# Values projected beside the tasks of the pair ahead and transposed, queries and keys in turn, FFN's rows behind its residuals

## What is computed

```python
proj = h @ w_in                      # queries, keys and values of all 16 heads, and the forget logits
s = einsum('bqhd,bkhd->bhqk', q, k) / sqrt(64) + F_q - F_k      # F: running sum of log_sigmoid
p = softmax(where(kpos <= qpos, s, NEG))
x = x + g1 * (einsum('bhqk,bkhd->bqhd', p, v) @ w_o)
...
u = h @ w_up                                                     # 1024 -> 5632
gate, val = split(conv_b + sum(conv_w[j] * shifted(u, j) for j in range(3)))
x = x + g2 * ((silu(gate) * val) @ w_down)
```

## Time and profile before

| what | us |
|---|---|
| median of 3 runs | 2390.47 (2387.61 to 2393.91) |
| the profiled execution | 2388.44 |
| its span, first to last instruction | 2386.6 |
| PE busy in it | 2293.8 (96%) |
| DVE, ACT, POOL busy | 1541.0, 1146.3, 1209.4 |

### The profile page before, as it was taken

How to read it: one execution, slowest core, us unless ns; L and a number is a source line. 1 busy time by engine, 2 the same in 40 slices (tenths; PEclk the granted TensorE clock), 3 DMA queues, 4 the chain that set the end, 5 groups by cost and what they waited for, 6 DMA issues and landing times.

```text
span 2386.6 us, 30699 instructions
## 1 busy us (share of the span) xinstructions
PE 2293.8 (96%) x10986; PEld 1909.2 (80%) x10986; DVE 1541.0 (65%) x2536; ACT 1146.3 (48%) x1993; POOL 1209.4 (51%) x1641
## 2 busy tenths in 40 slices
PE   5999999998998999999999999989999999999998
PEld 4778788787877888888888878987778888888886
DVE  6565756658789677777776577882775555555556
ACT  5365664746255333333333496771553333333333
POOL 1501312133557666667666562214376666666663
PEclk9999999999999999999999999989999999999999
DMA  6211211114621333344332323233111111111112
GB/s 264 63 49 36 69 38 50 45 45 176 222 96 58 111 124 124 124 128 124 121 123 93 106 71 78 54 109 130 36 45 53 54 53 53 54 53 54 54 54 80
DMA packets 69082, 207.20 MB, mean 87 GB/s; under 512 B 7729, under 2 KB 8369, under 8 KB 68802
## 3 DMA queue, kind: packets, MB, share of 16 engines
q1 hardware_dynamic: 35248, 121.13, 15.7%
q10 hardware_dynamic: 33682, 84.11, 11.0%
HBM read 186.92 MB, written 16.32 MB: 85 GB/s over the span
## 4 chain that ended last, share of the span: by engine, by line
PE 80%; DVE 12%; ACT 4%; issue 2%; DMA 1%; SPq 0%; ACTq 0%; DVEq 0%
PE bank L1063 50%; PE bank L753 18%; PE bank L892 1%; PE bank L918 1%; PE bank L953 1%; PE bank L928 1%; PE bank L1280 1%; PE bank L955 1%; PE bank L954 1%; PE bank L1220 1%; DVE ada_raw L1974 1%; DMA ada_raw<-in_ada_t 1%; ACT H L1405 1%; DVE bank L2064 1%; DVE PL L2090 1%
## 5 line engine op out<-in xcount | busy, mean ns | idle before, releaser
L1063 PE MATMUL bank<-H,w_spl 128*128 128x512 f32 x3552 | 824.2, 390 | 8.2 <-DVE X L2285 6.5
L1063 PEld LDWEIGHTS bank<-H,w_spl 128*128 128x128 f32 x3552 | 667.6, 188 | 151.8 <-DVE X L2285 9.3
L651 POOL TENSOR_TENSOR w_spl<-w_raw,w_spl 128x256 fp32r<-128x256 f32 x688 | 551.3, 829 | 408.1 <-ACT w_spl L1647 406.7
L1063 PE MATMUL bank<-TB,w_spl 128*128 128x512 f32 x2112 | 493.6, 390 | 1.6 <-DVE TB L2245 1.6
L753 PE MATMUL bank<-H,w_spl 128*128 128x512 f32 x1920 | 481.3, 397 | 5.2 <-DVE H L2424 2.5
L1063 PEld LDWEIGHTS bank<-TB,w_spl 128*128 128x128 f32 x2112 | 396.1, 188 | 85.8 <-issue 3.4
L753 PEld LDWEIGHTS bank<-H,w_spl 128*128 128x128 f32 x1920 | 354.7, 190 | 76.2 <-DVE H L2424 2.9
L1647 ACT ACTIVATE w_spl<-w_raw 128x512 fp32r<-128x512 f32 x328 | 196.4, 624 | 348.0 <-PE bank L1063 291.8
L590 POOL TENSOR_TENSOR pace<-one_s 128x1 f32<-128x1 f32 x49 | 13.7, 280 | 578.9 <-PE bank L918 352.4
L2276 DVE TENSOR_TENSOR bank<-bank,sU 128x512 f32<-128x512 f32 x80 | 55.9, 699 | 280.7 <-PE bank L1063 280.7
L2285 DVE SCALAR_TENSOR_TENSOR X<-bank,mods,X 128x1024 f32<-128x1024 f32 x160 | 204.7, 1279 | 34.6 <-PE bank L1063 33.9
(11 more groups left out here) (203 smaller groups left out, 3367.7 us busy)
## 6 DMA issues: line engine op xcount, KB each, us to landing
w_raw<-in_w_stream SPq DMA_DIRECT2D x184, 512.0 KB, 3.7
ada_raw_f<-in_ada_t ACTq DMA_DIRECT2D x136, 256.0 KB, 2.9
ada_raw<-in_ada_t SPq DMA_DIRECT2D x8, 1024.0 KB, 18.8
negF<-scratch_f ACTq DMA_DIRECT2D x16, 512.0 KB, 3.8
ada_raw_o<-in_ada_t ACTq DMA_DIRECT2D x4, 2048.0 KB, 8.1
ada_raw_o<-in_ada_t ACTq DMA_DIRECT2D x4, 1536.0 KB, 8.0
Hf<-scratch_o ACTq DMA_DIRECT2D x9, 512.0 KB, 4.5
X<-in_x_t SPq DMA_DIRECT2D x4, 1024.0 KB, 11.7
```

Source lines behind the costliest of these rows:

```text
L651: last = pool.tensor_tensor(block_at(layer, b, 1, q, q + 256), src[:, q:q + 256], block_at(layer, b, 0, q, q + 256).bitcast(F32), ALU.subt ...
L1063: last = pe.matmul(dst, block_at(layer, b, x, k * P, k * P + P), mov(y), start=(start and x + y == 0), stop=(stop and x == 1), skip_group_ ...
```

## The change

**Values.** They are projected for each pair from the third on, with the weights as the stationary operand: `v_step(r, i)` is half of a product of 128 value columns by 256 rows of the sequence, 12 matmuls of 256 columns, and stands in task 14 + i of the pair before (i from 0 to 7). The result is transposed: ACT copies a quarter of 256 rows out of PSUM (`copy_vt`, a task behind), PE transposes it in two (`turn_v`, two tasks behind), and ACT and DVE split it (`v_high`, `v_low`, three tasks behind). The weight tiles are laid out for it, one more stationary tile per pair in place of two moving ones per group. Nothing stands between groups any more.

**Queries and keys.** From the third pair on the halves come in turn: queries and keys of the first half of the sequence, then of the second. A table `FILL` is the same for every pair but the first. All heads have their maxima beside the tasks of the head before (`MAX_T`).

**Heads' outputs.** They may come into H when the last values are projected, not the last keys; `HEADS_SPLITS` and `OUT_A_BESIDE` start later.

**ConvFFN.** In pair 2 the four rows of factors go behind the gating and the third residual, the first residual stands right behind the first taps; in pair 3 the first row goes behind a sum. ACT's two loads for it stand at the end of pair 2.

In the diff comments and empty lines are left out.

```diff
-MAX_V = [0, 0, 0, 3, 3, 3, 3, 0]
-MAX_K = (1, 4, 7)
-MAX_T = [[2, 1, 1, 1, 1, 1, 1, 2, 2, 0, 0, 0], [0, 0, 2, 1, 2, 1, 2, 1, 2, 1, 0, 0]]
-MAX_T.append(MAX_T[0])
-V_EARLY = 3
-V_TASK = 4 * NT - V_EARLY
+MAX_T = [[2, 1, 1, 1, 1, 1, 1, 2, 2, 0, 0, 0], [1, 1, 1, 1, 1, 1, 2, 1, 2, 1, 0, 0]]
+MAX_T += MAX_T
 PREFACE = 16
-FILL_1 = [2] * 16
-FILL_1_FIRST = [2] * 8
-FILL_2 = [0] * (2 * NT) + [1, 1, 1, 1, 1, 2] * 2 + [3, 2, 2, 2] * 2
+FILL = [3, 2, 2, 3, 2, 2, 2, 2, 2, 3, 3, 3, 3]
+FILL_FIRST = [2] * 8
+V_TASK = 14
...
-HEADS_SPLITS = {22: 0, 24: 1, 26: 2, 28: 3, 30: 4, 32: 5, 42: 6}
+HEADS_SPLITS = {26: 0, 27: 1, 29: 2, 31: 3, 33: 4, 35: 5, 42: 6}
...
-OUT_A_BESIDE = {25: (0,), 28: (1,), 31: (2,), 34: (3,), 37: (4,), 40: (5,), 44: (6,)}
+OUT_A_BESIDE = {28: (0,), 30: (1,), 32: (2,), 34: (3,), 37: (4,), 40: (5,), 44: (6,)}
...
-    return (n % 2, n // 2) if n < 4 else (n % 4 // 2, n % 2)
+    return (n % 4 // 2, n % 2) if n // 4 == 1 else (n % 2, n % 4 // 2)
 def qk_pos(n):
     pair = n // 4
-    if pair == 0:
-        return 2 + n % 2
-    return 6 * (pair // 2) + 4 * (pair % 2) + n % 4 // 2
+    return 2 * (pair == 0) + 3 * pair + (pair == 1) + qk_part(n)[0]
 def qk_steps(g, T):
-    if T < 2 * NT:
-        fill, done, first = (FILL_1, 0, 8 * g + 4) if g else (FILL_1_FIRST, PREFACE, 4)
-    elif g < NG - 1:
-        fill, done, first = FILL_2, 0, 8 * g + 8
-    else:
+    r, t = 2 * g + T // (2 * NT) + 1, T % (2 * NT)
+    fill, done = (FILL, 0) if r > 1 else (FILL_FIRST, PREFACE)
+    if 2 * r >= NH or t >= len(fill):
         return []
-    if T >= len(fill):
-        return []
-    a = done + sum(fill[:T])
-    return [(first + i // KT, i % KT) for i in range(a, a + fill[T])]
+    a = done + sum(fill[:t])
+    return [(4 * r + i // KT, i % KT) for i in range(a, a + fill[t])]
+def v_beside(g, T):
+    q, t = divmod(4 * NT * g + T, 2 * NT)
+    return [(q + 1, t - V_TASK)] if 0 <= t - V_TASK < 8 and 1 <= q < NH // 2 - 1 else []
+def v_quarter(g, T):
+    return [(r, i // 2) for r, i in v_beside(g, T) if i % 2]
...
-                            sp.wait_ge(qk_ps, 8 * NG)
+                            sp.wait_ge(v_ps, 8 + 4 * (NH // 2 - 2))
...
-            def v_step(g, tt, between=True):
...
+            def v_step(r, i):
+                qd = i // 2
+                if i == 0:
+                    pe.wait_ge(w_ready, 3 * r + 3)
+                if i in (0, 2):
+                    pe.wait_ge(qk_lo, 2 * (4 * r + 3 + qd))
+                elif i % 2 == 0:
+                    pe.wait_ge(v_lo, 8 + 4 * (r - 2) + qd - 1)
+                last = product(bank(6 + qd % 2, 0, 256), w_tile(3 * r + 2), h_cols(256 * qd, 256),
+                               range(4 * (i % 2), 4 * (i % 2) + 4))
+                if i % 2:
+                    last.then_inc(v_ps, 1)
+            def turn_v(r, qd):
+                pe.wait_ge(vt_copy, 4 * (r - 2) + qd + 1)
+                for j in range(2):
+                    last = pe.transpose(bank(6 + qd % 2, 256 + j * P, 256 + j * P + P), vt[:, j * P:j * P + P], id_f[:])
+                last.then_inc(vt_ps, 1)
...
-                for tt in range(V_EARLY, 8) if g else ():
-                    v_step(g, tt)
-                    if tt < V_EARLY + LAG:
-                        value(g - 1, 4 * NT - LAG + tt - V_EARLY)
                 for T in range(4 * NT):
                     hl, t = T // NT, T % NT
                     score(g, T)
                     if T >= LAG:
                         value(g, T - LAG)
-                    maxima = list(maxima_at(MAX_T[hl], t)) if hl < 3 else []
+                    elif g:
+                        value(g - 1, 4 * NT - LAG + T)
+                    for r, qd in v_quarter(g, T - 2):
+                        turn_v(r, qd)
+                    maxima = list(maxima_at(MAX_T[hl], t)) if 4 * g + hl + 1 < NH else []
                     steps = qk_steps(g, T)
                     while maxima or steps:
                         if maxima:
                             maximum(4 * g + hl + 1, maxima.pop(0))
                         if steps:
                             qk_step(*steps.pop(0))
-                    if hl < 3 and t == 10:
+                    for r, tt in v_beside(g, T):
+                        v_step(r, tt)
+                    if 4 * g + hl + 1 < NH and t == 10:
                         turn_max(4 * g + hl + 1)
-                    if g < NG - 1 and T >= V_TASK:
-                        v_step(g + 1, T - V_TASK, False)
                     if g == NG - 1:
...
+            def copy_vt(r, qd):
+                act.wait_ge(v_ps, 8 + 4 * (r - 2) + qd + 1)
+                act.wait_ge(vt_ps, 4 * (r - 2) + qd)
+                nc.scalar.activation(vt[:], bank(6 + qd % 2, 0, 256), ACT.Copy).then_inc(vt_copy, 1)
+            def v_high(r, qd):
+                act.wait_ge(vt_ps, 4 * (r - 2) + qd + 1)
+                act.wait_ge(pv_ps, 2 * NT * (r - 1))
+                nc.scalar.activation(V[:, 2 * qd:2 * qd + 2, r % 2, 0:3:2, :],
+                                     bank(6 + qd % 2, 256, HALF).rearrange("p (t e d) -> p t e d", t=2, e=2),
...
+                    for r, qd in v_quarter(g, T - 1):
+                        copy_vt(r, qd)
+                    for r, qd in v_quarter(g, T - 3):
+                        v_high(r, qd)
...
-                    if p == NORMAL:
-                        load(0)
                     act.wait_ge(c_sum, n + 2)
                     tap(p, 0, pair(0))
-                    if p == NORMAL:
-                        load(1)
...
                         next_high(p, 3)
+                    if p == NORMAL:
+                        load(0)
+                        load(1)
...
+            def v_low(r, qd):
+                dve.wait_ge(v_hi, 8 + 4 * (r - 2) + qd + 1)
+                V_.tensor_tensor(V[:, 2 * qd:2 * qd + 2, r % 2, 3:6:2, :],
+                                 bank(6 + qd % 2, 256, HALF).rearrange("p (t e d) -> p t e d", t=2, e=2),
+                                 V[:, 2 * qd:2 * qd + 2, r % 2, 0:3:2, :].bitcast(F32), ALU.subtract).then_inc(v_lo, 1)
...
+                    for r, qd in v_quarter(g, T - 3):
+                        v_low(r, qd)
...
-                    step(0)
+                    if p > NORMAL + 1:
+                        step(0)
                     if p > NORMAL:
                         sum_of(p, 1, 1, 0, ALU.add, sU)
+                    if p == NORMAL + 1:
+                        step(0)
                     if p % 2 == 0 and p > NORMAL:
                         low_part((p - 2) // 2, 0)
                         low_part((p - 2) // 2, 1)
-                    step(1)
                     if p > NORMAL:
+                        step(1)
                         step(2)
                     sum_of(p, 4, 3, 1, ALU.add, sU)
                     if p > NORMAL:
                         step(3)
                     taps(p, 0, pair(0))
                     if p == NORMAL:
-                        step(2)
-                        step(3)
+                        half_residual(p, 0)
                     step(4)
...
-                    half_residual(p, 0)
+                    half_residual(p, int(p == NORMAL))
                     taps(p, 1, pair(2))
-                    half_residual(p, 1)
+                    if p > NORMAL:
+                        half_residual(p, 1)
                     step(6)
                     gated(p)
                     half_residual(p, 2)
+                    if p == NORMAL:
+                        for i in range(4):
+                            step(i)
                     step(7)
```

116 lines of the change are left out of this document (40 added, 76 removed).

## The result

| | us |
|---|---|
| changed kernel, median of 9 runs | 2402.16 (2395.66 to 2406.5) |
| kernel before, median of 9 runs beside it | 2390.47 (2387.61 to 2394.07) |
| ratio, 95% interval | 1.0048 (1.0039 to 1.0058) |
| predicted | 2398 (2385 to 2406) |

The change makes the kernel slower by 11.7 us. The time lies inside the range and 4 us above the forecast. The profiled execution of the changed kernel is its slowest, 2406.5 with a span of 2404.7, and stands 18.1 above that of before where the medians stand 11.7 apart. So sizes are taken from the trace for each place, and from medians for each kernel.

A forecast was written before the change was run, and what follows sets the result against it. PE, busy 2293.8 of 2386.6 us, was taken to bound the kernel. Attention +12.5 and ConvFFN -3.8 and -1.7 gave +7.0 on 2388.4, 2395.4; with the runs' median 2.0 higher, 2397.5, taken as 2398, range 2385 to 2406.

The forecast's parts named there:

- Part 1: Attention: 24 waits worth 18.1 us go, but next pairs' first scores still wait for `max_rows`, 2 us over 6 pairs.
- Part 2: Attention: what comes; value steps in tasks 18 and 20 wait for V's splits, 2.1 and 1.7 late, 22.7 us in all.
- rival A: Attention: value steps hide the splits, so those waits don't come and only transposes do; faster, 2375; chance 0.13.
- Transposes, +4.5: Attention: 48 new transposes on PE, 0.125 us each, a quarter hidden at the pair's end; 4.5 us, bounds 1.5 and 13.
- The last pair, +2: Attention's last pair: POOL's split of tile 26 starts later, so `o_low` and PE are late; 2 us, between 0 and 4.
- The first pair, -0.6: Attention's first pair: maxima only spread better, one extra wait goes; 0.6 us off, between 0 and 2.
- Part 3: ConvFFN: residual waits go; gains of 3.8 us in layer 0 and 1.7 in layer 1.
- give-back: Layer 0's ConvFFN, pair 3: ACT's copies come 1.7 and 2.4 us late behind loads, taking 4.1 from the 7.9 gained.
- Layer 1: ConvFFN without rows of factors: its two residual waits, 1.4 and 0.3 us, go; 1.7 us won, between 0 and 2.
- B: No change that can be told: waits a third shorter, or layer 0's loads give nothing back; 2390 to 2394; chance 0.23.
- D: Layer 0's ConvFFN gains nothing net, as the same rows come late in pair 3; 2402; chance 0.52 together with the forecast.
- C: Clearly slower: half clock after every task 18's wait, 10 us more, 2408; decides from a printed wait of about 1.9; chance 0.12.

The follow-up runs named there:

- early release: Changed kernel with the release of a pair's value weights moved from the next pair's first score to the score of task 22: 2398.2 us, ratio 1.0032.
- loads late: Changed kernel with ACT's three load instructions for pair 3 of layer 0 put one place later, behind copies: 2394.2 us, ratio 1.0019.
- transposes twice: Changed kernel with each pair of value transposes issued twice, 48 more transposes: 2403.98 us, ratio 1.0065.
- DVE only: Changed kernel with DVE's low part of V ahead of its task's row maxima, ACT's value instructions still behind the exponential: 2403.64 us, ratio 1.0058.
- splits first: Changed kernel with ACT's value instructions ahead of their task's exponential and DVE's low part of V ahead of the row maxima: 2383.75 us, ratio 0.9974.

## Why the prediction was right, and where it was off

- **Part 1, 24 waits gone, -18.1, and +2 for the first scores.** Right. From 168 to 568 us no wait of those is left, and a first score is 0.28 late, as forecast (0.3): 1.7 us.
- **Part 2, the splits in tasks 18 and 20, +22.7.** The mechanism is right in each step. The chain of 3.3 us from the score to the value step was 3.07 (218.19 to 221.26), PE's own 1.2 was 1.26: 1.81 late for 2.1, and 1.35 for 1.7 in task 20, together 19.0. As printed the second is 1.25, under the 1.6 to 2.0 that was to show it. The sum took full steps of ACT where instructions overlap by 0.1 (the copy of the quarter took 0.26 from start to start, not 0.39). "ACT's list decides", as the argument against rival A had it, was half of it: DVE's maxima were as late.
- **A wait that the prediction lacked.** The step ahead of task 18's, in task 14, waits for the low part of the queries, 0.53 late, six times: 3.2 us. It said that no other value step would wait. It fills what the twelve fell short, so the six pairs came to +12.2 (10.6 without the fall of the clock) where the terms gave 11.1. Two errors met there.
- **Transposes, +4.5.** 0.108 to 0.113 each, 5.2 to 5.4 for 48, and those in front of the pair's end hidden: right, and not 13.
- **The last pair, +2.** Right in cause, small in size: a wait of 2.8 and a half clock behind it, 3.8 us by the timeline; the early release won 4.0 of median and 2.5 of this stretch.
- **The first pair, -0.6.** It can't be told: that pair took 51.3 for 51.6, and from 48.7 to 51.6 over the twelve profiled executions.
- **Part 3, ConvFFN, -5.5.** The 7.9 for the wait that goes is right, 7.8. The step that failed is the give-back, forecast at 4.1 (1.7 and 2.4 late) and measured at 9.4. Its first half stands: ACT's copy of U 0 was forecast to end at 782.2 of before's time, which is 801.0 here (this place lies 18.8 later), and ended at 801.35. The second half was worked out with 3.5 to 3.9 us for the data of pair 3's first row, read from the earlier trace rows, where the load stood behind the same broadcast. They took 6.6, with two of SyncE's weight loads beside them; the sum took the transfer's time over from a place where those came later. So the copy began at 807.9 where 787.4 + 18.8 less its length, 805.6, was forecast, and PE waited 4.1 as printed. The half clock behind it, 2.8 us, was in no term. Why the transfer was slower stays open. That ACT's loads stand ahead of the copies is shown: moving them won 8.0 by medians. Layer 1 was -2.1 for -1.7.
- **Sum.** Behind the start the traces have +15.1 where the forecast had +7.0 (15.9 + 1.3 - 2.1); by medians +11.7 for +7.5. The excess is the ConvFFN (4.7), the last pair (1.8), one fall of the clock in attention (1.5) and the first pair's 0.6, less 0.5 in the six pairs. The number came near because the direction and the largest terms were right; that it missed by only 4 us is in part luck, since in attention two errors of over 3 us cancelled.
- **Rivals.** A did not come; it took both engines' order to bring its case, and then it was 2383.75, not 2375, since the first scores and the waits for QS stay, and the last pair and layer 0's ConvFFN were as in the changed kernel. B did not come. D came, layer 0's ConvFFN gains nothing; that its 2402 is the median measured is luck, as the trace has +15.1 where D makes +10.8. C came in part. Of the executions profiled with the wait of task 18 at 1.64, the changed kernel, loads late, transposes twice and early release each show one of six pairs 1.5 us longer than the others, and DVE only shows none: 4 of 30, not every task 18.
- **The rows under C.** Two readings were wrong. The half clock at the earlier trace rows's wait of 1.96 did not last 3.4 us; that was the width of the window in the earlier trace rows. It began before the wait ended and lasted 6.8:

```profile
142.40:149.20 6.80, 5.57 (x21) 5.37 (x22) 3.70 (x7) 3.59 (x7) 0.00 (x0) 0.50 0.31 109
```

The falls in attention did last 3.4, so the price of 1.7 was near by luck. And "about 1.9 up" does not decide. The kernel before itself has a wait of 1.92 with full clock behind it:

```profile
70.99 0.50 PE L753 MATMUL bank<-H,w_spl 128*128 128x512 f32 x1 [1.92 <-DVE V L2025]
```

```profile
71.00:76.00 5.00, 5.00 (x22) 4.11 (x23) 3.46 (x9) 2.02 (x7) 4.92 (x10) 1.00 0.21 47
```

All twelve profiled executions have this wait, 1.90 to 1.93 long, and in eight of them a half clock begins behind it (0.66 from 71 to 76 us in splits first).
